# Six query and key projections of a stick-breaking attention: hi and lo tokens as one 512-column moving operand

## The chip, the core and the metric

The kernel runs on one NeuronCore of a Trainium2 chip. The metric is the device time of one execution in microseconds (us), lower is better. Engines are named as the profile names them: PE (TensorE matmuls), PEld (its weight loads), DVE (VectorE), ACT (ScalarE), SP (the queue that issues the weight transfers).

## The reference

A first block works on `x` (256 tokens, 1024 wide); two further layers of another kind follow. All of it is fp32. The part that the change touches is the projection of the normalised tokens to queries and keys:

```python
h = rms_norm(x, g_mix[l])
proj = h @ w_in[l]
c_h, c_b, c_c, sq, sk, sv, xq, gate_pre = jnp.split(proj, split_idx, axis=-1)
...
# stick-breaking attention, 16 heads of 64
z = jnp.einsum("bhqd,bhkd->bhqk", qb, kb).astype(jnp.float32) * scale   # scale = 0.125
log_beta = jax.nn.log_sigmoid(z)
log_1mb = jnp.where(past, jax.nn.log_sigmoid(-z), 0.0)
between = lax.cumsum(log_1mb, axis=3, reverse=True) - log_1mb
a = jnp.where(past, jnp.exp(log_beta + between), 0.0)
```

## The kernel before, in words

**Products.** Every fp32 matmul is made of three products of rounded parts: hi weights with hi tokens, lo weights with hi tokens, hi weights with lo tokens. The weights arrive in pieces of 1024 rows by 256 output columns, called halves here and `h` in the code. A half is one transfer of 1 MB into one of two slots of `raw`. ACT rounds it to `w_hi` (line 360), DVE forms `w_lo = raw - w_hi` (line 840), each into one of four ring slots. `split(0, h + 4)` in both engines' loops does this four halves ahead. SP issues the transfer of half l when DVE has formed `w_lo` of half l-2 (line 290).

**Order.** Halves 0 to 3 give the values, 4 to 11 (`SQK` to `CC`) the queries and keys in turn (even: queries, odd: keys), 12 to 23 the convolution's inputs. Every engine has its own program written out by hand, a loop over `h` with what is to be done beside each half; semaphores tie them together. Halves 4 and 5 use the raw tokens `Q_hi`, `Q_lo` and are scaled by DVE afterwards; halves 6 to 11 use the normalised tokens `H_hi`, `H_lo`.

**One half of a query or key on PE** (`rows_first`, line 1516): the weights are the stationary operand, the tokens the moving one, 256 columns. For each of 2 groups of 128 outputs and 8 pieces of 128 inputs there are three matmuls of 256 columns, 48 in all. Both groups share one bank of PSUM, `gps[:, h % 3]`. PE starts half h once `evac` has reached h-2, that is when the half that last used the bank has been copied out.

**Leaving PSUM.** One ACTIVATE of 128x512 (`evac`, line 376) copies a finished half to `qs` or `ks`; it stands in ACT's program ahead of the split of half h+4. Of halves 4 and 5 DVE does the copy, and ACT only raises the count `evac` by a `sem_inc`.

**Wide halves elsewhere.** In the feed-forward parts `rows_wide` (lines 1553 and 1557) already takes hi and lo tokens as one moving operand of 512 columns (`R_both`), with two banks for a half. What belongs together is then in one bank: hi products in columns 0 to 255, the lo tokens' products in columns 256 to 511. ACT copies the latter out (line 448), DVE adds the former (line 1034).

Of the kernel before, what the change touches and what calls it, by code (L numbers as in the profile page):

```python
# [20 lines left out]
P = 128  # L21
# [53 lines left out]
def build(nc, mem_t, x_t, x, w1, w2, rows1, rows2, rows3, par1, par2, con1, con2, turns, out):  # L75
    with ExitStack() as ctx:
        def sb(name, shape, dt=F32):
            return ctx.enter_context(nc.sbuf_tensor(name, shape, dt))

        def sem(name):  # L80
# [4 lines left out]
        w_hi = sb("w_hi", [P, 4, HALF], F32R)  # L85
        w_lo = sb("w_lo", [P, 4, HALF], F32R)

        H_hi, H_lo = sb("H_hi", [P, KT, T], F32R), sb("H_lo", [P, KT, T], F32R)
        R_both = sb("R_both", [P, KT, 2, T], F32R)
        R_hi, R_lo = R_both[:, :, 0, :], R_both[:, :, 1, :]  # L90
        Q_hi, Q_lo = sb("Q_hi", [P, KT, T], F32R), sb("Q_lo", [P, KT, T], F32R)
# [69 lines left out]
        raw_loaded = [sem("raw_loaded0"), sem("raw_loaded1")]  # L161
        x_piece = [sem(f"x_piece{i}") for i in range(4)]
        w_piece = [sem(f"w_piece{i}") for i in range(8)]
        names = """zeros front_xlo qk_scaled front_g front_hi front_lo vs_var vs_log vs_scale mem_loaded x_loaded par_loaded cst_loaded con_loaded lpar_loaded out_stored
            hi_ready lo_ready gemm_done evac act_step dve_step pads
            nsq nsum nvar nlog nrow nt nhi nlo resid acc_ready sqsum rows_loaded gn_row_loaded
            t_sq t_var t_log t_z t_tr summed
# [59 lines left out]
        def up_bank(m):  # L227

            return gps[:, m + 1, :]

        def wide_bank(a, nt):

# [119 lines left out]
        def _(act):  # L352
# [15 lines left out]
            def bank(l, ringsize=3):  # L368
                return gps[:, l % ringsize, :]

            def two(ap):
                return ap.rearrange("p (a t) -> p a t", a=2)
# [245 lines left out]
            staged_n = 0  # L618
            for h in range(SQK, FFN1):
                ps = bank(h)  # L620
                if h < SQK + 2:
                    act.wait_ge(s["qk_scaled"], h - SQK + 1)
                    act.sem_inc(s["evac"], 1)
                elif h < CC:
                    i = (h - SQK) // 2
                    if h % 2 == 0:
                        evac(qs[:, 2 * i:2 * i + 2, :], two(ps), h + 1, scale=0.125)
                    else:
                        evac(ks[:, 2 * i:2 * i + 2, :], two(ps), h + 1)
                elif h < CH:  # L630
                    i = h - CC
                    evac(u[:, 2 * i:2 * i + 2, 2:T + 2], two(ps), h + 1)
                elif h < MK:

                    if staged_n >= 2:
                        act.wait_ge(s["staged_free"], staged_n - 1)
                    evac(staged[:, staged_n % 2, :], ps, h + 1)
                    staged_n += 1
                elif h < MV or XQ <= h < XQ + 4:
                    if h in heads_ends:  # L640
                        n = heads_ends.index(h)
                        act.wait_ge(s["hd_tr"], n)
                        for m in range(2):
                            evac(heads[:, m, :], bank(h - 1 + m), h + 1)
                        head_squares(n)
                elif h < XQ:
                    if (h - MV) % 2:
                        for m in range(2):
                            evac(chunk(vx, m, (h - MV) // 2), bank(h - 1 + m), h + 1)
                elif h < WO1:  # L650
                    if (h - 36) % 4 == 1:
                        for m in range(2):
                            act.wait_ge(s["gemm_done"], h + 1)
                            act.wait_ge(s["staged_free"], staged_n + m - 1)
                            act.activation(gate[:, m, :], bank(h - 1 + m), ACT.Sigmoid).then_inc(s["evac"], 1)
                    elif (h - 36) % 4 == 3:
                        for m in range(2):
                            act.wait_ge(s["staged_free"], staged_n - 1)
                            evac(staged[:, m, :], bank(h - 1 + m), h + 1)
                            staged_n += 1  # L660
                if h in (GATED["conv"] + 4, WO1):
                    for m in range(2):
                        j = int(h == WO1)
                        act.wait_ge(s["mg_tr"], 2 * j + m + 1)
                        act.activation(operand(Q_hi, m, j), four(merged_turned(m, j)), ACT.Copy)\
                           .then_inc(s["mg_hi"], 1)
                if h == WO1:
                    act.preload_act_table_set("natural_log_exp_and_others")
                if h == MEM0:

                    act.wait_ge(s["mem_loaded"], 16)
                    for a in range(2):
                        squares(B7, B5, 2 * a, 2 * a + 2, s["nsq"])
                if h == MEM0 + 2:
                    rms_start(1)
                if SB0 <= h <= SB0 + 18:
                    t = (h - SB0) // 2
                    if h % 2 == 0:
                        if t >= 2:
                            sb_out(t - 2)  # L680
                        if t < SB_PAIRS:
                            sb_full(t)
                    elif t >= 1:
                        sb_copy(t - 1)
                if h + 4 < FFN1 + 2:
                    split(0, h + 4)
                if SB0 <= h <= SB0 + 18:
                    t = (h - SB0) // 2
                    if t < SB_PAIRS:
                        if h % 2 == 0:  # L690
                            sb_logs(t)
                        else:
                            sb_exp(t)
                if MEM0 + 2 <= h < MEM0 + 6:
                    rms_hi(1, h - MEM0 - 2, B5, R_hi)
                if h in heads_ends:
                    head_log(heads_ends.index(h))
                if CV0 <= h < CV0 + 4:

                    i = h - CV0  # L700
                    act.wait_ge(s["gemm_done"], XQ)
                    act.wait_ge(s["conv_y"], i + 1)
                    act.activation(R_hi[:, 2 * i:2 * i + 2, :], y[:, 2 * i:2 * i + 2, :], ACT.Copy)\
                       .then_inc(s["cv_hi"], 1)
                if h == CV0 + 3:
                    act.wait_ge(s["cv_lo"], 4)
                x0 = X0
                if x0 + 2 <= h < x0 + 2 + X_HEADS:
                    cx_out(h - x0 - 2)
                if x0 + 1 <= h < x0 + 1 + X_HEADS:  # L710
                    cx_copy(h - x0 - 1)
                if x0 <= h < x0 + X_HEADS:
                    cx_exp(h - x0)
                if h == GATED["x"] - 1:
                    act.wait_ge(s["gemm_done"], h + 1)
                    act.wait_ge(s["cx_oe"], X_HEADS)
                    for i in range(4):
                        act.activation(Q_hi[:, 2 * i:2 * i + 2, :], ox[:, 2 * i:2 * i + 2, :], ACT.Copy)\
                           .then_inc(s["ox_hi"], 1)
# [114 lines left out]
        def _(dve):  # L834
# [386 lines left out]
            dve.memset(u[:, :, 0:2], 0.0).then_inc(s["pads"], 1)  # L1221
            staged_n = 0
            for h in range(SQK, FFN1):
                if SB0 <= h <= SB0 + 18:
                    t = (h - SB0) // 2
                    if h % 2 == 0:
                        if t >= 2:
                            sb_out(t - 2)
                        if t < SB_PAIRS:
                            sb_masked(t)  # L1230
                    elif t < SB_PAIRS:
                        sb_arg(t)
# [276 lines left out]
        def _(pe):  # L1509
# [25 lines left out]
            def rows_first(h0, l, bank_, op_hi, op_lo, split_count=None):  # L1535
# [6 lines left out]
                        ins = rows_part(l, bank_, op_hi, op_lo, (nt,), range(KT))  # L1542
                ins.then_inc(s["gemm_done"], 1)

            def rows_wide(h0, l, a):

                r = ring(l)
                pe.wait_ge(s["lo_ready"], h0 + (l + 1))
                for nt in range(2):
                    b = wide_bank(a, nt)  # L1550
                    for k in range(KT):
                        c = k * 256 + nt * P
                        pe.matmul(b, w_hi[:, r, c:c + P], R_both[:, k, :, :].rearrange("p i t -> p (i t)"),  # L1553
                                  start=(k == 0), stop=False, skip_group_check=True)
                    for k in range(KT):
                        c = k * 256 + nt * P
                        ins = pe.matmul(b[:, 0:T], w_lo[:, r, c:c + P], R_hi[:, k, :],  # L1557
                                        start=False, stop=(k == KT - 1), skip_group_check=True)
                ins.then_inc(s["gemm_done"], 1)

            def tokens_part(l, out, m, g, op_hi, op_lo, start=False, stop=False, ks=range(4),
# [254 lines left out]
                              start=(m == 0 and j == 0), stop=(j == 1), skip_group_check=True)  # L1816
            sum_tiles(B5, (0, 1), aps[:, 3, 0:T], True, True).then_inc(s["nsum"], 1)
            for h in range(2, FFN1):
                if 3 <= h < WO1:
                    pe.wait_ge(s["evac"], h - 2)  # L1820
                if h < SQK:
                    tokens_half(0, h, h % 2, (2, 0), Q_hi, Q_lo, 1 if h == 2 else None)
                elif h < SQK + 2:
                    rows_first(0, h, h % 3, Q_hi, Q_lo)
                elif h < CC:
                    rows_first(0, h, h % 3, H_hi, H_lo, (s["nhi"], s["nlo"], 0, (1, 2, 3, 4)) if h == SQK + 2 else None)
                elif h < MK:
                    rows_first(0, h, h % 3, H_hi, H_lo)
                elif h < XQ:
# [344 lines left out]
```

## Time and profile before

| | |
|---|---|
| time, median of 3 runs | 1202.31 us (1202.1 to 1202.74) |
| time of the profiled execution | 1201.94 us |
| its span in the profile | 1200.2 us, 16502 instructions |
| PE busy | 1191.0 us (99%) |
| PEld, DVE, ACT busy | 1013.7 us (84%), 802.1 us (67%), 616.5 us (51%) |
| granted clock of TensorE, mean | 0.999 of full |
| DMA, mean | 183 GB/s |

The span is what the profiled execution's instructions cover. A matmul's row starts where the matmul starts, but its end is modelled and overlaps the next one's start, so a matmul's price in a stream is the distance between two starts and not its duration.

### The profile page before, as it was taken

The page shows a single profiled execution, that of the slowest core. Times are in us where ns is not written, and L with a number is a line of the kernel's source. Part 1 is how long each engine was busy: PE and PEld are TensorE (multiplying, and loading weights), DVE is VectorE, ACT ScalarE, POOL GpSimd, SP SyncE. Part 2 cuts the span into 40 slices and gives each one's busy share as a digit, 9 for nine tenths or more (in the row PEclk, how much of TensorE's full clock was granted, in tenths as well). Part 3 has the DMA queues.
Part 4 walks back from the last instruction along what each step waited for, and adds up shares of the span by engine and source line. Part 5 has one row for each costly group of instructions (what it writes and reads, how often), then busy time and mean ns, then how long its engine had stood idle before and what let it go on. Part 6 is the DMA issues. An engine that isn't in the chain of part 4 may idle for free.

```text
span 1200.2 us, 16502 instructions
## 1 busy us (share of the span) xinstructions
PE 1191.0 (99%) x6500; PEld 1013.7 (84%) x6500; DVE 802.1 (67%) x952; ACT 616.5 (51%) x769; POOL 3.5 (0%) x10
## 2 busy tenths in 40 slices
PE   9999999999999999999999999999999999999997
PEld 7999988888888888888888888888888888888886
DVE  6787986564656676656369697665675878766556
ACT  6567675564444555344356545443436654544441
POOL 0000000000000000000000000000000000000000
PEclk9999999999999999999999999999999999999999
DMA  7655354543555365555264446555536444565550
GB/s 263 227 190 176 135 182 148 207 172 140 220 200 190 115 236 201 184 203 182 105 246 176 149 177 214 207 199 186 191 124 246 169 155 176 188 228 180 194 192 36
DMA packets 34490, 219.25 MB, mean 183 GB/s; under 512 B 4080, under 2 KB 6144, under 8 KB 9088
## 3 DMA queue, kind: packets, MB, share of 16 engines
q1 hardware_dynamic: 32704, 215.26, 50.2%
q0 software_dynamic: 640, 2.11, 0.5%
q10 hardware_dynamic: 1088, 1.05, 0.3%
q8 instruction: 43, 0.70, 0.2%
q14 instruction: 15, 0.12, 0.0%
HBM read 217.34 MB, written 1.06 MB: 182 GB/s over the span
## 4 chain that ended last, share of the span: by engine, by line
PE 97%; DVE 1%; DMA 1%; ACT 0%; issue 0%; SPq 0%; DVEq 0%
PE gps L1516 14%; PE gps L1553 13%; PE gps L1571 11%; PE gps L1580 11%; PE gps L1573 11%; PE aps L1573 8%; PE aps L1571 8%; PE aps L1580 8%; PE gps L1557 7%; DMA raw<-w 1%; PE aps L1598 1%; PE aps L1755 1%; PE aps L1779 1%; PE aps L1929 0%; PE aps L1717 0%; PE gps L1941 0%
## 5 line engine op out<-in xcount | busy, mean ns | idle before, releaser
L840 DVE TENSOR_TENSOR w_lo<-raw,w_hi 128x2048 fp32r<-128x2048 f32 x194 | 444.2, 2291 | 234.9 <-ACT w_hi L360 234.2
L360 ACT ACTIVATE w_hi<-raw 128x2048 fp32r<-128x2048 f32 x194 | 371.5, 1916 | 214.2 <-PE aps L1580 96.7
L1553 PE MATMUL gps<-R_both,w_hi 128*128 128x512 f32 x672 | 167.9, 392 | 0.0
L1571 PE MATMUL aps<-w_hi,Q_hi 128*128 128x512 f32 x416 | 162.2, 390 | 0.0
L1573 PE MATMUL aps<-w_lo,Q_hi 128*128 128x512 f32 x416 | 162.2, 390 | 0.0
L1553 PEld LDWEIGHTS gps<-R_both,w_hi 128*128 128x128 f32 x672 | 122.2, 189 | 22.7
L1571 PE MATMUL gps<-w_hi,H_hi 128*128 128x512 f32 x288 | 114.8, 399 | 0.0
L1573 PE MATMUL gps<-w_lo,H_hi 128*128 128x512 f32 x288 | 112.4, 390 | 0.0
L1580 PE MATMUL aps<-w_hi,Q_lo 128*128 128x512 f32 x416 | 111.5, 390 | 0.0
L1516 PE MATMUL gps<-H_hi,w_hi 128*128 128x256 f32 x416 | 110.0, 286 | 0.0
L1516 PE MATMUL gps<-H_hi,w_lo 128*128 128x256 f32 x416 | 108.5, 283 | 0.0
L1557 PEld LDWEIGHTS gps<-R_both,w_lo 128*128 128x128 f32 x672 | 91.7, 190 | 6.6
L1557 PE MATMUL gps<-R_both,w_lo 128*128 128x256 f32 x672 | 93.7, 282 | 0.0
L1573 PEld LDWEIGHTS aps<-w_lo,Q_hi 128*128 128x128 f32 x416 | 78.2, 188 | 15.7
L1580 PEld LDWEIGHTS aps<-w_hi,Q_lo 128*128 128x128 f32 x416 | 77.9, 188 | 16.0
L1571 PEld LDWEIGHTS aps<-w_hi,Q_hi 128*128 128x128 f32 x416 | 78.2, 188 | 15.5
L1516 PE MATMUL gps<-H_lo,w_hi 128*128 128x256 f32 x416 | 83.1, 283 | 0.0
L1516 PEld LDWEIGHTS gps<-H_hi,w_hi 128*128 128x128 f32 x416 | 79.6, 191 | 3.2 <-issue 3.0
L448 ACT ACTIVATE staged<-gps 128x256 f32<-128x256 f32 x84 | 27.7, 382 | 101.6 <-PE gps L1557 101.6
L1516 PEld LDWEIGHTS gps<-H_hi,w_lo 128*128 128x128 f32 x416 | 79.7, 192 | 0.1
L1580 PE MATMUL gps<-w_hi,H_lo 128*128 128x512 f32 x288 | 77.7, 391 | 0.0
L1571 PEld LDWEIGHTS gps<-w_hi,H_hi 128*128 128x128 f32 x288 | 54.1, 188 | 14.3 <-issue 3.5
(252 smaller groups left out, 1561.6 us busy)
## 6 DMA issues: line engine op xcount, KB each, us to landing
raw<-w SPq DMA_DIRECT2D x194, 1024.0 KB, 4.8
B<-rows SPq DMA_DIRECT2D x4, 1024.0 KB, 4.5
raw<-w SPq DMA_DIRECT2D x8, 256.0 KB, 6.8
B<-turns POOLq DMA_DIRECT2D x4, 512.0 KB, 7.2
B<-x_t ACTq DMA_DIRECT2D x4, 256.0 KB, 5.6
B<-mem_t SPq DMA_DIRECT2D x1, 1024.0 KB, 8.7
B<-x SPq DMA_DIRECT2D x1, 1024.0 KB, 6.9
out<-B SPq DMA_DIRECT2D x4, 256.0 KB, 2.0
```

The source lines that it names most:

```text
L360: act.activation(w_hi[:, ring(l), :], raw[:, raw_slot(l), :], ACT.Copy)\
L448: act.activation(staged[:, a, nt * T:(nt + 1) * T], wide_bank(a, nt)[:, T:2 * T], ACT.Copy)\
L840: dve.tensor_tensor(w_lo[:, ring(l), :], raw[:, raw_slot(l), :], w_hi[:, ring(l), :].bitcast(F32), ALU.subtract)\
L1516: return pe.matmul(gps[:, bank_, nt * T:(nt + 1) * T], w[:, r, c:c + P], op[:, k, :], start=start, stop=stop, skip_group_check=True)
L1553: pe.matmul(b, w_hi[:, r, c:c + P], R_both[:, k, :, :].rearrange("p i t -> p (i t)"), start=(k == 0), stop=False, skip_group_check=True)
L1557: ins = pe.matmul(b[:, 0:T], w_lo[:, r, c:c + P], R_hi[:, k, :], start=False, stop=(k == KT - 1), skip_group_check=True)
L1571: pe.matmul(out, x, w_hi[:, r, c], start=(start and k == ks[0]), stop=False, skip_group_check=resumed)
L1573: pe.matmul(out, x, w_lo[:, r, c], start=False, stop=False, skip_group_check=resumed)
L1580: ins = pe.matmul(out, op_lo[:, 4 * g + k, rows], w_hi[:, r, c], start=False, stop=(stop and k == ks[-1]), skip_group_check=resumed)
L1598: ins = pe.transpose(turned(m, j)[:, k * P:(k + 1) * P], chunk(src, m, j)[:, k * P:(k + 1) * P], ident)
L1755: ins = pe.matmul(aps[:, h % 2, t * T:(t + 1) * T], qx[:, 2 * h + j, t * P:(t + 1) * P], kx[:, 2 * h + j, :], start=(j == 0), stop=(j == 1))
L1779: ins = pe.matmul(aps[:, 2, j * T:(j + 1) * T], vx[:, m, c:c + P], xpt[:, m * T:(m + 1) * T], start=(m == 0), stop=(m == 1))
```

## The change

`H_hi` and `H_lo` become the two parts of one tile `H_both`, laid out as `R_both` is. Halves 6 to 11 no longer run through `rows_first` but through `scores_wide`: 16 matmuls of 512 columns (hi weights with hi and lo tokens) and 16 of 256 (lo weights with hi tokens). A half has two banks: even halves `gps` 0 and 1, odd halves 2 and 3. ACT copies the lo columns of each bank to `qs` or `ks` (two ACTIVATEs of 128x256, count `qk_low`), then DVE adds the hi columns of the bank (two SCALAR_TENSOR_TENSORs of 128x256, count `qk_wide`). PE waits on `qk_wide` before it writes a pair of banks again.

```diff
+        H_both = sb("H_both", [P, KT, 2, T], F32R)
+        H_hi, H_lo = H_both[:, :, 0, :], H_both[:, :, 1, :]
...
 (ACT)       for h in range(SQK, FFN1):
                 ps = bank(h)
+                if SQK + 3 <= h <= CC:
+                    act.wait_ge(s["qk_wide"], 2 * (h - SQK - 2))
+                    act.sem_inc(s["evac"], 1)
                 if h < SQK + 2:
                     act.wait_ge(s["qk_scaled"], h - SQK + 1)
                     act.sem_inc(s["evac"], 1)
                 elif h < CC:
-                        evac(qs[:, 2 * i:2 * i + 2, :], two(ps), h + 1, scale=0.125)
-                        evac(ks[:, 2 * i:2 * i + 2, :], two(ps), h + 1)
+                    act.wait_ge(s["gemm_done"], h + 1)
+                    for nt in range(2):
+                        act.activation(qk_tile(h, nt), qk_bank(h, nt)[:, T:2 * T], ACT.Copy,
+                                       scale=(0.125, 1.0)[h % 2]).then_inc(s["qk_low"], 1)
...
 (DVE)       for h in range(SQK, FFN1):
+                if SQK + 2 <= h < CC:
+                    for nt in range(2):
+                        dve.wait_ge(s["qk_low"], 2 * (h - SQK - 2) + nt + 1)
+                        dve.scalar_tensor_tensor(qk_tile(h, nt), qk_bank(h, nt)[:, 0:T], (0.125, 1.0)[h % 2],
+                                                 qk_tile(h, nt), ALU.mult, ALU.add).then_inc(s["qk_wide"], 1)
...
 (PE)
+            def scores_wide(h):
+                pe.wait_ge(s["lo_ready"], h + 1)
+                if h == SQK + 2:
+                    for k in range(KT):
+                        if k % 2 == 0:
+                            pe.wait_ge(s["nlo"], k // 2 + 1)
+                        for nt in range(2):
+                            wide_hi(h, qk_bank(h, nt), nt, k, H_both)
+                    for nt in range(2):
+                        ins = wide_lo(h, qk_bank(h, nt), nt, H_both)
+                else:
+                    for nt in range(2):
+                        for k in range(KT):
+                            wide_hi(h, qk_bank(h, nt), nt, k, H_both)
+                        ins = wide_lo(h, qk_bank(h, nt), nt, H_both)
                 ins.then_inc(s["gemm_done"], 1)
...
-                if 3 <= h < WO1:
+                if SQK + 2 <= h < SQK + 4:
+                    pe.wait_ge(s["evac"], h - 1)
+                elif SQK + 4 <= h <= CC:
+                    pe.wait_ge(s["qk_wide"], 2 * (h - SQK - 3) if h < CC else 10)
+                elif 3 <= h < WO1:
                     pe.wait_ge(s["evac"], h - 2)
...
-                    rows_first(0, h, h % 3, H_hi, H_lo, (s["nhi"], s["nlo"], 0, (1, 2, 3, 4)) if h == SQK + 2 else None)
+                    scores_wide(h)
```

**DVE's program around half 6.** `B` stands for `qs` and `ks` here and for the squares of the memory tokens, `w_lo` is the low part of the weights. Before, from the memset that follows the split of half 7; the two splits are those of halves 8 and 9:

```order
L1221 MEMSET B 128x8x2 [waits nlo]
L840 TENSOR_TENSOR w_lo<-raw,w_hi 128x2048 [waits hi_ready] x2
L868 TENSOR_TENSOR B<-B 128x1024 [waits nsq]
L870 TENSOR_TENSOR B<-B 128x512 [waits dve_step]
L840 TENSOR_TENSOR w_lo<-raw,w_hi 128x2048 [waits hi_ready] x2
```

And of the change at the same place:

```order
L1233 MEMSET B 128x8x2 [waits nlo]
L852 TENSOR_TENSOR w_lo<-raw,w_hi 128x2048 [waits hi_ready] x2
L1239 SCALAR_TENSOR_TENSOR B<-gps,B 128x256 [waits qk_low] x2
L880 TENSOR_TENSOR B<-B 128x1024 [waits nsq]
L882 TENSOR_TENSOR B<-B 128x512 [waits dve_step]
L852 TENSOR_TENSOR w_lo<-raw,w_hi 128x2048 [waits hi_ready]
L1239 SCALAR_TENSOR_TENSOR B<-gps,B 128x256 [waits qk_low] x2
L852 TENSOR_TENSOR w_lo<-raw,w_hi 128x2048 [waits hi_ready]
```

The sum of half 6 stands behind the splits of halves 8 and 9, that of half 7 behind the split of half 10; each later sum also stands ahead of the split of the half four on.

**PE's program, halves 7 to 9.** Before; the three waits are the starts of halves 7, 8 and 9, and the rows between them, which repeat one pattern, are left out:

```order
L1516 MATMUL gps<-H_hi,w_hi 128x256 [waits lo_ready,evac]
...
L1516 MATMUL gps<-H_hi,w_hi 128x256 [waits lo_ready,evac]
...
L1626 MATMUL aps<-B,cst 128x256 [waits sqsum,nrow]
...
L1516 MATMUL gps<-H_hi,w_hi 128x256 [waits lo_ready,evac]
```

And of the change, halves 7 and 8:

```order
L1565 MATMUL gps<-H_both,w_hi 128x512 [waits lo_ready,evac]
L1565 MATMUL gps<-H_both,w_hi 128x512 x7
L1572 MATMUL gps<-H_both,w_lo 128x256 x8
L1565 MATMUL gps<-H_both,w_hi 128x512 x8
L1572 MATMUL gps<-H_both,w_lo 128x256 x8
L1565 MATMUL gps<-H_both,w_hi 128x512 [waits lo_ready,qk_wide]
L1565 MATMUL gps<-H_both,w_hi 128x512 x7
L1572 MATMUL gps<-H_both,w_lo 128x256 x8
L1565 MATMUL gps<-H_both,w_hi 128x512 x8
L1572 MATMUL gps<-H_both,w_lo 128x256 x8
```

The start of half 8 hangs on `qk_wide` of half 6 where it hung on `evac` of half 5.

## Rows read from the trace of the kernel before

**Rows 1.** The page: busy time of each engine; chain that ended last, by engine

```profile
PE 1191.0 (99%) x6500; PEld 1013.7 (84%) x6500; DVE 802.1 (67%) x952; ACT 616.5 (51%) x769; POOL 3.5 (0%) x10
PE 97%; DVE 1%; DMA 1%; ACT 0%; issue 0%; SPq 0%; DVEq 0%
```

**Rows 2.** Waits of PE: us in total, times, longest

```profile
PE aps L1808 <- DVE staged L1182: 1.2, 1, 1.2
PE gps L1571 <- DVE w_lo L840: 0.3, 1, 0.3
```

**Rows 3.** Timeline of PE: starts of halves 6 and 8; what follows halves 8 and 10

```profile
43.84 0.28 PE L1516 MATMUL gps<-H_hi,w_hi 128*128 128x256 f32 x1
...
55.36 0.28 PE L1516 MATMUL gps<-H_hi,w_hi 128*128 128x256 f32 x1
...
61.12 1.02 PE L1626 MATMUL aps<-B,cst 128*128 128x256 f32 x4
...
73.58 0.50 PE L1704 MATMUL aps<-B 64*128 64x128 f32 x4
```

**Rows 4.** Timeline of PE: a wide half of the feed-forward part

```profile
420.88 1.98 PE L1553 MATMUL gps<-R_both,w_hi 128*128 128x512 f32 x8
422.69 1.12 PE L1557 MATMUL gps<-R_both,w_lo 128*128 128x256 f32 x8
423.64 2.00 PE L1553 MATMUL gps<-R_both,w_hi 128*128 128x512 f32 x8
```

**Rows 5.** Timeline of DVE: splits of halves 9 to 13, one sum of squares

```profile
54.48 2.29 DVE L840 TENSOR_TENSOR w_lo<-raw,w_hi 128x2048 fp32r<-128x2048 f32 x1 [1.36 <-ACT w_hi L360]
56.85 1.23 DVE L868 TENSOR_TENSOR B<-B 128x1024 f32<-128x1024 f32 x1
...
60.04 2.29 DVE L840 TENSOR_TENSOR w_lo<-raw,w_hi 128x2048 fp32r<-128x2048 f32 x1 [1.23 <-ACT w_hi L360]
64.41 2.29 DVE L840 TENSOR_TENSOR w_lo<-raw,w_hi 128x2048 fp32r<-128x2048 f32 x1 [2.07 <-ACT w_hi L360]
...
70.22 2.29 DVE L840 TENSOR_TENSOR w_lo<-raw,w_hi 128x2048 fp32r<-128x2048 f32 x1
...
73.82 2.29 DVE L840 TENSOR_TENSOR w_lo<-raw,w_hi 128x2048 fp32r<-128x2048 f32 x1
```

**Rows 6.** Timeline of ACT: splits of halves 8 and 9, evacuation of half 6

```profile
48.87 1.92 ACT L360 ACTIVATE w_hi<-raw 128x2048 fp32r<-128x2048 f32 x1 [4.77 <-DMA raw<-w]
52.53 1.92 ACT L360 ACTIVATE w_hi<-raw 128x2048 fp32r<-128x2048 f32 x1 [1.74 <-DMA raw<-w]
54.35 0.58 ACT L376 ACTIVATE B<-gps 128x512 f32<-128x512 f32 x1
```

**Rows 7.** SP's issue of half 9's transfer; time to landing of raw's transfers

```profile
47.70 0.33 SPq L290 DMA_DIRECT2D raw<-w  x1
DMA to landing us min/median/max: 4.3/4.8/9.3
```

**Rows 8.** Timeline: two evacuations and two additions of a wide half

```profile
429.85 0.66 ACT L448 ACTIVATE staged<-gps 128x256 f32<-128x256 f32 x2
432.21 0.75 DVE L1034 TENSOR_TENSOR staged<-staged,gps 128x256 f32<-128x256 f32 x2
```

**Rows 9.** Timeline: a split of DVE, and PE's first two matmuls behind it

```profile
18.25 2.29 DVE L840 TENSOR_TENSOR w_lo<-raw,w_hi 128x2048 fp32r<-128x2048 f32 x1
...
20.59 0.50 PE L1571 MATMUL gps<-w_hi,Q_hi 128*128 128x512 f32 x1 [0.27 <-DVE w_lo L840]
20.93 0.40 PE L1573 MATMUL gps<-w_lo,Q_hi 128*128 128x512 f32 x1
```

**Rows 10.** The last matmul; then stretches: busy times, PEclk, DMA share, GB/s

```profile
1192.79 0.39 PE L1580 MATMUL aps<-w_hi,Q_lo 128*128 128x512 f32 x1
1194.00:1196.00 2.00, 0.00 (x0) 0.00 (x0) 1.86 (x7) 0.41 (x2) 0.00 (x0) 1.00 0.00 0
1196.00:1198.00 2.00, 0.00 (x0) 0.00 (x0) 1.67 (x3) 0.00 (x0) 0.00 (x0) 0.83 0.35 131
```

More of the change, by code:

```diff
@@ L86, in build @@
         w_lo = sb("w_lo", [P, 4, HALF], F32R)
-        H_hi, H_lo = sb("H_hi", [P, KT, T], F32R), sb("H_lo", [P, KT, T], F32R)
+        H_both = sb("H_both", [P, KT, 2, T], F32R)
+        H_hi, H_lo = H_both[:, :, 0, :], H_both[:, :, 1, :]
         R_both = sb("R_both", [P, KT, 2, T], F32R)
@@ L163, in build @@
         w_piece = [sem(f"w_piece{i}") for i in range(8)]
-        names = """zeros front_xlo qk_scaled front_g front_hi front_lo vs_var vs_log vs_scale mem_loaded x_loaded par_loaded cst_loaded con_loaded lpar_loaded out_stored
+        names = """qk_low qk_wide zeros front_xlo qk_scaled front_g front_hi front_lo vs_var vs_log vs_scale mem_loaded x_loaded par_loaded cst_loaded con_loaded lpar_loaded out_stored
             hi_ready lo_ready gemm_done evac act_step dve_step pads
@@ L229, in up_bank, with qk_tile, qk_bank @@
             return gps[:, m + 1, :]
+        def qk_tile(h, nt):
+            return (qs, ks)[h % 2][:, 2 * ((h - SQK) // 2) + nt, :]
+        def qk_bank(h, nt):
+            return gps[:, 2 * (h % 2) + nt, :]
         def wide_bank(a, nt):
@@ L624, in _ @@
                 elif h < CC:
-                    i = (h - SQK) // 2
-                    if h % 2 == 0:
-                        evac(qs[:, 2 * i:2 * i + 2, :], two(ps), h + 1, scale=0.125)
-                    else:
-                        evac(ks[:, 2 * i:2 * i + 2, :], two(ps), h + 1)
+                    act.wait_ge(s["gemm_done"], h + 1)
+                    for nt in range(2):
+                        act.activation(qk_tile(h, nt), qk_bank(h, nt)[:, T:2 * T], ACT.Copy,
+                                       scale=(0.125, 1.0)[h % 2]).then_inc(s["qk_low"], 1)
                 elif h < CH:
@@ L1543, in rows_first, with wide_hi, wide_lo @@
                 ins.then_inc(s["gemm_done"], 1)
+            def wide_hi(l, b, nt, k, both):
+                c = k * 256 + nt * P
+                pe.matmul(b, w_hi[:, ring(l), c:c + P], both[:, k, :, :].rearrange("p i t -> p (i t)"),
+                          start=(k == 0), stop=False, skip_group_check=True)
+            def wide_lo(l, b, nt, both):
+                for k in range(KT):
+                    c = k * 256 + nt * P
+                    ins = pe.matmul(b[:, 0:T], w_lo[:, ring(l), c:c + P], both[:, k, 0, :],
+                                    start=False, stop=(k == KT - 1), skip_group_check=True)
+                return ins
             def rows_wide(h0, l, a):
-                r = ring(l)
                 pe.wait_ge(s["lo_ready"], h0 + (l + 1))
@@ L1551, in rows_wide @@
                     for k in range(KT):
-                        c = k * 256 + nt * P
-                        pe.matmul(b, w_hi[:, r, c:c + P], R_both[:, k, :, :].rearrange("p i t -> p (i t)"),
-                                  start=(k == 0), stop=False, skip_group_check=True)
-                    for k in range(KT):
-                        c = k * 256 + nt * P
-                        ins = pe.matmul(b[:, 0:T], w_lo[:, r, c:c + P], R_hi[:, k, :],
-                                        start=False, stop=(k == KT - 1), skip_group_check=True)
+                        wide_hi(l, b, nt, k, R_both)
+                    ins = wide_lo(l, b, nt, R_both)
+                ins.then_inc(s["gemm_done"], 1)
+            def scores_wide(h):
+                pe.wait_ge(s["lo_ready"], h + 1)
+                if h == SQK + 2:
+                    for k in range(KT):
+                        if k % 2 == 0:
[9 more added lines that the diff above has]
+                        ins = wide_lo(h, qk_bank(h, nt), nt, H_both)
                 ins.then_inc(s["gemm_done"], 1)
```

## The prediction

> **What bounds the kernel now.** I read the page first: PE is busy for 99% of the span and makes up 97% of the chain that ended last, the chain of waits back from the last instruction [rows 1]. Then PE's waits: the longest is 1.2 us at the very start, the next 0.3 us [rows 2], and the last matmul starts at 1192.79 [rows 10], so the rest of the span is a tail of DVE and the output. PE is a gapless stream. Whatever makes this stream shorter or puts a hole into it moves the end by as much, since nothing behind it waits for anything else. So two questions remain: how much shorter six halves become, and whether PE has to wait where it did not.
>
> **What the matmuls give.** The timeline shows half 6 starting at 43.84, half 8 at 55.36 and the next work after half 8 at 61.12 [rows 3]: three halves in 17.28 us, 5.76 us each, or 120 ns for each of the 48 matmuls of 256 columns. A wide half is in the trace too, in the feed-forward part: eight matmuls of 512 columns from 420.88 to 422.69 (226 ns each), eight of 256 until 423.64 (119 ns each) [rows 4]. One group of 128 outputs takes 2.76 us, a half 5.52 us. The change turns each pair of 256-column matmuls (240 ns) into one of 512 (226 ns), 16 times per half: 0.24 us a half, 1.44 us over six halves. That is the whole possible gain, because the number of streamed columns stays at 12,288.
>
> Here a rule speaks against the change. In the Trainium skill, "TensorE: Matmul & The Clock Gate", section "Wait — 56ns, not 53.3ns?", a warm matmul's distance to the next is given as its columns at 2.4 GHz and about 2.5 ns. By that, merging two matmuls saves only 2.5 ns, an estimate of 0.24 us for all 96 merges, and the end would be 1.2 us later than by the rows. The rows differ from it (120 ns for 256 columns), so the rows decide here.
>
> **What the new wait costs.** PE may start half 8 only when DVE has added up half 6, because both use banks 0 and 1. Before, half 8 needed the copy of half 5, long done. I follow each engine.
>
> PE: halves 6 and 7 take 5.52 us each from 43.84, so PE is ready for half 8 at 54.88. (Half 7 also waits for ACT's `sem_inc`, which stands behind the split of half 8, 48.87 to 50.79 [rows 6]. Taken at the start of that split it costs nothing; taken at its end half 7 would run from 50.8 to 56.4. The wait that follows ends later than both, so the choice does not move half 8.)
>
> ACT: its copy of half 6 stands behind the split of half 9, which in turn waited for its transfer until 52.53; the copy started at 54.35 [rows 6]. That transfer was issued at 47.70 and took 4.8 us, the median [rows 7]. None of this hangs on how fast PE is, so it stays. Two copies of 128x256 take 0.66 us [rows 8] for the 0.58 us of one [rows 6], so the first half's columns are there near 54.7, the second's near 55.0.
>
> DVE: in its order the sum of half 6 stands behind the split of half 9, from 54.48 to 56.77 [rows 5]. Only then come the two new instructions. The nearest operation in the trace is the addition of a bank's half to a copy in SBUF in the wide halves, 0.75 us for two [rows 8]. It can't be free, as DVE works in program order; the dear end is a DVE instruction of twice the two's size, 128x1024 in 1.23 us [rows 5], half a us more. I take 0.75, the row of the nearest operation and shape. So the sum is ready at 57.5.
>
> PE restarts about 0.05 us behind that: after an earlier wait, on a split of DVE that ended at 18.25 + 2.29 = 20.54, it started at 20.59, and the second matmul came 0.34 us behind the first instead of 0.23 [rows 9], another 0.11 us. Half 8 so runs as if it had begun at 57.68 instead of 55.36: 2.3 us later than before, and PE stands idle for 2.7 us.
>
> **Does it happen again?** Half 9 needs the sum of half 7, which stands behind DVE's split of half 10. That split waits for ACT and, through it, a transfer; it stays at 60.04 to 62.33 [rows 5], since the sum of half 6 and the sums of squares (56.85 before, 0.8 us later now) fill idle time ahead of it. The sum of half 7 is ready at 63.1. PE reaches half 9 at 57.68 + 5.52 + 0.9 for the matmuls at line 1626 [rows 3] = 64.1: 1.0 us to spare. Half 10: split at 64.41, ends 66.7, sum ready 67.4, PE there at 69.6. Half 11: the split at 70.22 ends 72.5, 0.75 later now, and the sum 0.75 after that makes 74.0; PE is there at 76.0, behind the scores that followed half 10 at 73.58 [rows 3]. Half 12: the split at 73.82 ends at 76.1, three sums of 0.75 make 78.4, PE comes at 81.5. No further stall. These six pairs of sums add 4.5 us to DVE, which is idle 1 to 2 us ahead of most splits here [rows 5]; that idle time is the cover. If it were gone, `w_lo` of the halves 10 to 15 would be late, but each is ready several us before PE needs it. ACT's waits for `qk_wide` ask for sums of one half earlier, done by then. SP's queue moves only where `w_lo` moves, from half 12 on by 0.75 us, with three halves of PE's time to spare. The rounded tokens of half 6 are no new wait: lo parts are written before PE's stretch for the later pieces.
>
> **The sum.** +2.3 us at half 8, then four halves (8 to 11) shorter by 0.24: -0.96. The gain of halves 6 and 7 is inside the stall. Together +1.3 us. The profiled execution was 1201.94 (span 1200.2 and 1.7 around it), so it would be 1203.3; the median of the runs shown is 0.4 higher, and 1202.31 + 1.3 = 1203.6 is my forecast. It is 0.11% slower, and about 0.2% (2.4 us) is what a measurement of this kernel can tell from no change.
>
> **The rivals.**
> - *No stall, the full gain.* If the copy and the sum of half 6 were done by 54.9, the end would be 1.44 us earlier: 1200.9. For it speaks only that PE never waited here before; against it that DVE's split alone ends at 56.77. The transfer of half 9 would have to land 2.6 us sooner, in 2.2 us, with 4.3 the shortest of the trace [rows 7]. Chance 0.08, mostly for an error in my reading of the order.
> - *A later transfer (slower than can be taken for no change).* The stall's end hangs on the landing of half 9, then 1.92 us of ACT, 2.29 us of DVE and the sum, all in a row: each us by which it lands later is a us more. From 1.1 us on, a landing after 5.9 us, the result passes +2.4 us; the longest in the trace is 9.3 us [rows 7], which would give +5.8, or 1208.1. A late half 10 would use up the 1.0 us of half 9 likewise. Against it: this very transfer was at the median. At 1.4 us of lateness it is 1205.0. Chance 0.09.
> - *The clock falls in the stall.* The granted clock is full until 1196 at least, 2.8 us behind the end of the last matmul (1193.18), and lower in the stretch after [rows 10]. A hole of 2.7 us in a busy stream is just short of what is shown to be harmless. If the clock fell to 1.2 GHz, a half of 5.52 us at that level would cost 5.5 us more: 1209. The Trainium skill ("TensorE: Matmul & The Clock Gate", section "HAM oscillation — how this bites in real kernels") tells of kernels whose clock drops in waits between groups of matmuls. Chance 0.03.
> - *The merge gives nothing* (spacing as bound by loads or reads here): the stall without the 0.96, +2.3 us, 1204.6. Against it: the same operand shapes, in the feed-forward part [rows 4]. Chance 0.04.
>
> **How the numbers follow.** The forecast has 0.74; 0.02 stay for something faster that I do not see. The forecast's own range comes from a landing at 4.3 us (-0.5), the dear end of the sum (+0.5) and half a us of spread either way: 1202.6 to 1204.6. For 8 in 10 I reach a little to both sides, toward the full gain's 1200.9 at the low end and to a transfer that is 1.4 us late at the high end: 1201.3 to 1205.0. Faster by over 0.2% would need 2.4 us where 1.44 is the whole gain: only the unseen 0.02. Slower by over 0.2%: the late transfer, the clock, and 0.01 for the upper edge of the last rival, 0.13. The rest is 0.85.
>
> **What would show it.** In the changed kernel's profile: starts of the new 512-column matmuls 226 ns apart; one PE wait of 2.5 to 3 us at half 8, released by DVE's sum, near 57.5; no wait at halves 9 to 12; the scores after half 10 about 1.5 us later than 73.58; the end 1.3 us later. I am wrong if DVE's sum of half 6 precedes 56.7, if PE waits at half 9 or 11 too, or if PE finds idle time later in which the delay vanishes.

## The result

The changed kernel takes 1204.97 us in the median of 11 runs (1203.18 to 1209.06), the kernel before 1202.31 us (1201.84 to 1202.74, also 11 runs). The medians are 2.7 us apart, 0.22%, where 1.3 us or 0.11% was forecast. The ratio over all runs is 1.0024, with a 95% interval of 1.0016 to 1.0031. The kernel is slower, by more than the noise, where a smaller loss was forecast and "no change that can be told" had the best chance. The profiled execution took 1205.2 us with a span of 1203.4 us, 3.2 us more than the span of before.

The page, busy times and the chain that ended last, which answer to [rows 1]:

```profile
PE 1191.3 (99%) x6404; PEld 1009.7 (84%) x6404; DVE 805.9 (67%) x964; ACT 616.6 (51%) x775; POOL 3.5 (0%) x10
PE 93%; DMA 3%; DVE 2%; ACT 1%; issue 0%; SPq 0%; DVEq 0%; ACTq 0%
```

PE has 96 matmuls fewer (16 merges in each of six halves), DVE 12 instructions more, ACT 6 more. The chain stays on PE for less of the span, 93% where it was 97%; transfers are 3% where they were 1%, DVE and ACT together 3% where they were 1%. So somewhere PE waited for them. The view of PE's waits (us in total, times, longest) says where, against [rows 2]:

```profile
PE gps L1565 <- DVE B L1239: 2.3, 1, 2.3
PE aps L1851 <- DVE staged L1194: 1.2, 1, 1.2
```

One new wait of any size, on DVE's sum (line 1239), once. (Three short ones, 1.0 us together, end before 21 us, in code that the change leaves alone; half 6 starts 0.1 us later than before.) PE's timeline around it, from half 6 on, as [rows 3] show it for before:

```profile
43.94 3.82 PE L1565 MATMUL gps<-H_both,w_hi 128*128 128x512 f32 x16
47.59 2.08 PE L1572 MATMUL gps<-H_both,w_lo 128*128 128x256 f32 x16
49.50 2.00 PE L1565 MATMUL gps<-H_both,w_hi 128*128 128x512 f32 x8
...
57.57 2.54 PE L1565 MATMUL gps<-H_both,w_hi 128*128 128x512 f32 x8 [2.32 <-DVE B L1239]
59.91 1.91 PE L1572 MATMUL gps<-H_both,w_lo 128*128 128x256 f32 x8
61.62 2.43 PE L1565 MATMUL gps<-H_both,w_hi 128*128 128x512 f32 x8
63.88 1.11 PE L1572 MATMUL gps<-H_both,w_lo 128*128 128x256 f32 x8
64.84 1.02 PE L1669 MATMUL aps<-B,cst 128*128 128x256 f32 x4
...
68.49 2.00 PE L1565 MATMUL gps<-H_both,w_hi 128*128 128x512 f32 x8
...
71.28 2.00 PE L1565 MATMUL gps<-H_both,w_hi 128*128 128x512 f32 x8
...
74.08 2.00 PE L1565 MATMUL gps<-H_both,w_hi 128*128 128x512 f32 x8
...
76.96 0.50 PE L1747 MATMUL aps<-B 64*128 64x128 f32 x4
```

Half 8 starts at 57.57, as forecast, and then takes 7.27 us (to 64.84) where a wide half takes 5.59 us (two groups of outputs, as from 68.49 over 71.28 to 74.08). The reason is in the view by stretches (its columns: length, busy times of PE, PEld, DVE, ACT and POOL, then the granted clock, DMA share and GB/s):

```profile
58.00:59.00 1.00, 1.00 (x6) 0.81 (x5) 0.96 (x2) 1.00 (x1) 0.00 (x0) 1.00 0.70 180
59.00:60.00 1.00, 1.00 (x5) 0.77 (x4) 0.71 (x2) 1.00 (x3) 0.00 (x0) 0.54 1.03 434
60.00:61.00 1.00, 1.00 (x7) 1.00 (x6) 1.00 (x1) 0.17 (x1) 0.00 (x0) 0.50 0.96 401
61.00:62.00 1.00, 1.00 (x5) 0.95 (x5) 1.00 (x2) 0.12 (x1) 0.00 (x0) 0.50 0.11 41
62.00:63.00 1.00, 1.00 (x5) 0.77 (x4) 0.62 (x2) 1.00 (x1) 0.00 (x0) 0.75 0.00 0
63.00:64.00 1.00, 1.00 (x7) 0.82 (x5) 0.17 (x1) 0.80 (x1) 0.00 (x0) 1.00 0.80 147
```

After the 2.3 us hole PE worked on at full clock for 1.5 us and then at 1.2 GHz, the lower of the two levels, for 3.4 us (a mean of 0.54 over 1 us is 0.92 us at 0.5, one of 0.75 is 0.5 us: 0.92 + 1 + 1 + 0.5). Half of that is lost: 1.7 us. Before, the clock was full here, and PE had no hole:

```profile
57.00:60.00 3.00, 3.00 (x27) 3.00 (x26) 1.77 (x2) 1.91 (x2) 0.00 (x0) 1.00 0.82 265
```

What held the sum back, in the chain of this kernel over the hole:

```profile
52.61 1.93 ACT w_hi L369
...
54.56 2.29 DVE w_lo L852
56.85 0.68 DVE B L1239 x2
...
57.57 2.54 PE gps L1565 x8
```

The split of half 9 on ACT, then on DVE, then the two instructions of the sum, then PE. The account of the span: half 8 starts 57.57 - 55.36 = 2.2 us later, the lower clock takes 1.7 us, and halves 8 to 11 are shorter by 0.17 us each, 0.7 together. That makes 3.2 us, and 3.2 is measured between the two profiled executions. (The medians are 2.7 us apart; the profiled execution of before was one of its faster ones.)

### The profile page after: what moved, and what is told of

Its sections match the earlier page's. It is cut to its first block, busy times and chain, and to the rows that moved or that the text cites. A ratio compares the mean times of both kernels' runs of the same rounds, so it can differ in the third digit from the quotient of the medians.

```text
span 1203.4 us, 16334 instructions
## 1 busy us (share of the span) xinstructions
PE 1191.3 (99%) x6404; PEld 1009.7 (84%) x6404; DVE 805.9 (67%) x964; ACT 616.6 (51%) x775; POOL 3.5 (0%) x10
## 4 chain that ended last, share of the span: by engine, by line
PE 93%; DMA 3%; DVE 2%; ACT 1%; issue 0%; SPq 0%; DVEq 0%; ACTq 0%
PE gps L1565 14%; PE gps L1614 11%; PE gps L1616 10%; PE gps L1623 10%; PE gps L1533 9%; PE aps L1616 8%; PE aps L1614 8%; PE aps L1623 8%; PE gps L1572 7%; DMA raw<-w 3%; DVE w_lo L852 1%; ACT w_hi L369 1%; PE aps L1641 1%; PE aps L1798 1%; PE aps L1822 1%; PE aps L1976 0%
## 5 line engine op out<-in xcount | busy, mean ns | idle before, releaser
L1533 PE MATMUL gps<-H_both,w_hi 128*128 128x256 f32 x640 | 119.1, 285 | 0.0
L1614 PE MATMUL gps<-w_hi,H_both 128*128 128x512 f32 x288 | 114.8, 399 | 0.0
L1616 PE MATMUL gps<-w_lo,H_both 128*128 128x512 f32 x288 | 112.5, 390 | 0.0
L1533 PEld LDWEIGHTS gps<-H_both,w_hi 128*128 128x128 f32 x640 | 100.8, 191 | 2.8 <-issue 2.3
L1533 PE MATMUL gps<-H_both,w_lo 128*128 128x256 f32 x320 | 83.5, 283 | 0.0
L1623 PE MATMUL gps<-w_hi,H_both 128*128 128x512 f32 x288 | 77.7, 392 | 0.0
L1614 PEld LDWEIGHTS gps<-w_hi,H_both 128*128 128x128 f32 x288 | 54.1, 188 | 14.3 <-issue 3.5
L1616 PEld LDWEIGHTS gps<-w_lo,H_both 128*128 128x128 f32 x288 | 54.1, 188 | 10.6
L1623 PEld LDWEIGHTS gps<-w_hi,H_both 128*128 128x128 f32 x288 | 53.6, 188 | 11.2 <-DVE H_both L924 0.2
```

What stands on the lines that cost most here:

```text
L1533: return pe.matmul(gps[:, bank_, nt * T:(nt + 1) * T], w[:, r, c:c + P], op[:, k, :], start=start, stop=stop, skip_group_check=True)
L1614: pe.matmul(out, x, w_hi[:, r, c], start=(start and k == ks[0]), stop=False, skip_group_check=resumed)
L1616: pe.matmul(out, x, w_lo[:, r, c], start=False, stop=False, skip_group_check=resumed)
L1623: ins = pe.matmul(out, op_lo[:, 4 * g + k, rows], w_hi[:, r, c], start=False, stop=(stop and k == ks[-1]), skip_group_check=resumed)
```

## Experiments

Two questions were open. Is the loss the hole and the clock and nothing else? And does the clock fall because PE stands idle, or because of something in the wide matmuls? The runs of one batch share 27 runs of the kernel before: median 1202.36 us in the first batch (e1 to e4), 1202.29 us in the second (e5 to e7). Where nothing else is said, an experiment has 11 runs. Ratios and intervals are those of the runs, and so differ a little from the ratio of the medians.

**e2_hole_filled: PE busy during the wait.**

```diff
+FILL = 10
...
                 elif SQK + 4 <= h <= CC:
+                    if h == SQK + 4:
+                        for i in range(FILL):
+                            pe.matmul(aps[:, 1, :], H_both[:, 0, 0, 0:P],
+                                      H_both[:, 0, :, :].rearrange("p i t -> p (i t)"),
+                                      start=True, stop=True, skip_group_check=True)
                     pe.wait_ge(s["qk_wide"], 2 * (h - SQK - 3) if h < CC else 10)
```

> The changed kernel, with ten more matmuls of 512 columns (results unused, a bank that nobody needs then) between halves 7 and 8, where PE stands idle. They take 2.26 us and the sum of half 6 comes when it came before. Theory (the fall of the clock is caused by PE's idle time): same wait for the sum, so half 8 starts at 57.6 as in the changed kernel, but no fall of the clock; 1203.6, with little spread between runs. Rival (the clock falls for another reason, or the loss is the wait alone): 1205.0 and the same spread as the changed kernel, 1203.2 to 1209.

Measured: 1203.57 us (1203.08 to 1207.41), ratio 1.0013 [1.0004, 1.0022]. PE's timeline:

```profile
55.02 2.46 PE L1868 MATMUL aps<-H_both 128*128 128x512 f32 x10
57.45 2.11 PE L1566 MATMUL gps<-H_both,w_hi 128*128 128x512 f32 x8
59.40 1.11 PE L1573 MATMUL gps<-H_both,w_lo 128*128 128x256 f32 x8
60.35 2.00 PE L1566 MATMUL gps<-H_both,w_hi 128*128 128x512 f32 x8
62.19 1.11 PE L1573 MATMUL gps<-H_both,w_lo 128*128 128x256 f32 x8
63.14 1.02 PE L1670 MATMUL aps<-B,cst 128*128 128x256 f32 x4
```

Half 8 starts where it did in the changed kernel (57.45), but takes 5.69 us and not 7.27, and by the medians the end comes 1.4 us sooner. Unused work makes the changed kernel faster, though it stays slower than the kernel before. Ten of these eleven runs lie at 1203.88 us or lower, ten of the eleven of the changed kernel at 1204.55 or higher, so the two do not overlap but for one run of each. The wait itself costs what was forecast for it; the rest of the loss goes when PE is kept busy, so it was PE's idle time that brought the fall of the clock. The spread, which was expected to be little, has one run at 1207.41 us with a mean granted clock of 0.996 (the others have 0.998 or 0.999). The kernel before has such a run too, one in the 27 of the second batch, at 1206.02 us and 0.995. So one outlier of that size says nothing of this hole.

**e3_narrow_hole_short and e4_narrow_hole_long: holes in the kernel before, nothing wide.**

```diff
                 if 3 <= h < WO1:
                     pe.wait_ge(s["evac"], h - 2)
+                if h == SQK + 4:
+                    pe.wait_ge(s["lo_ready"], SQK + 6)
```

That is e3. In e4 the last line is `pe.wait_ge(s["sqsum"], 2)`.

> The kernel before, with nothing wide; PE's half 8 waits for w_lo of half 9 (ready at 56.8, where half 8 began at 55.36), an artificial hole of 1.4 us. Theory (a hole costs its length, a fall of the clock comes on top only when the hole is long enough): 1202.3 + 1.4 = 1203.7 if the clock does not fall; with a fall 1205.4. Rival (a hole of this size is swallowed later by PE): 1202.3.

> The kernel before, with nothing wide; PE's half 8 waits for DVE's sums of squares (ready at 58.8), an artificial hole of 3.4 us. Theory: 1202.3 + 3.4 = 1205.7 without a fall of the clock, 1207.4 with one; I expect the fall in nearly every run, and a granted clock below that of the kernel before. Rival (the fall in the changed kernel comes from the wide matmuls and not from idle time): 1205.7 with the clock of the kernel before.

Measured: e3 1203.77 us (1203.36 to 1204.69), ratio 1.0011 [1.0002, 1.002]; e4 1207.62 us (five runs: 1205.96 to 1209.57), ratio 1.0042 [1.0028, 1.0056]. Chains of PE over the holes, first e3, then e4 (the view names no releaser for these two waits and calls them "issue"):

```profile
53.98 2.16 PE gps L1516 x18
56.13 1.36 issue
57.49 5.62 PE gps L1516 x45
```

```profile
56.47 3.42 issue
59.89 8.13 PE gps L1516 x44
```

And the stretches, the first of e3 behind its hole, then those of e4:

```profile
60.00:62.00 2.00, 2.00 (x19) 2.00 (x19) 1.10 (x1) 1.36 (x2) 0.00 (x0) 1.00 0.88 365
```

```profile
58.00:60.00 2.00, 0.11 (x1) 0.14 (x1) 1.97 (x3) 2.00 (x2) 0.00 (x0) 0.75 0.63 115
60.00:62.00 2.00, 2.00 (x10) 2.00 (x11) 1.99 (x1) 0.14 (x1) 0.00 (x0) 0.50 0.93 393
62.00:64.00 2.00, 2.00 (x11) 2.00 (x11) 0.00 (x0) 0.66 (x1) 0.00 (x0) 0.50 0.49 94
64.00:66.00 2.00, 2.00 (x12) 2.00 (x11) 0.72 (x1) 1.25 (x1) 0.00 (x0) 0.54 0.96 393
```

A hole of 1.36 us costs 1.4 us and the next half runs as ever. A hole of 3.4 us costs 5.3 us in the median; what is left beside its own length is 1.9 us. The profiled execution, the slowest of the five, shows where such a rest comes from: the clock is at the lower level from 59.0 to 65.8, and half 8 takes 8.45 us between starts (59.89 to 68.34) where a half takes 5.76, 2.7 us lost. Here the clock fell while PE still stood idle, 2.5 us behind the end of its last matmul. The one run at 1205.96 is 3.6 us above the kernel before and has a mean granted clock of 0.999, the other four have 0.996 to 0.998: in it the clock did not fall. So the fall needs no wide matmuls, and at this place it came behind holes of 2.3 and 3.4 us, not behind one of 1.4.

**e7_hole_part_filled: the hole cut to 1.3 us, the wait kept.** The edit of e2 with four matmuls for ten.

> The changed kernel with four unused matmuls of 512 columns (0.9 us) ahead of PE's wait at half 8, so that the hole shrinks from 2.5 to about 1.5 us while half 8 still starts at 57.6. Theory (what counts for the clock is how long PE is idle; 1.4 us in the narrow kernel did no harm): no fall, 1203.6, as with ten. Rival (any wait for the sum brings the fall, however long): 1205.0.

Measured: 1203.25 us (1202.93 to 1204.33), ratio 1.0005 [0.9996, 1.0014]. PE's timeline and the stretches of the profiled execution:

```profile
56.13 1.09 PE L1868 MATMUL aps<-H_both 128*128 128x512 f32 x4
58.56 2.14 PE L1566 MATMUL gps<-H_both,w_hi 128*128 128x512 f32 x8 [1.34 <-DVE B L1240]
```

```profile
57.00:60.00 3.00, 1.66 (x7) 1.20 (x7) 2.97 (x5) 3.00 (x5) 0.00 (x0) 1.00 0.28 57
60.00:63.00 3.00, 3.00 (x19) 2.62 (x18) 3.00 (x4) 0.58 (x3) 0.00 (x0) 1.00 0.70 295
```

A hole of 1.34 us in the changed kernel leaves the clock alone, like that of 1.36 in the narrow one. But this execution, the slowest of the eleven, has a fall elsewhere, near the start, where PE stands idle for a short time in some executions of these kernels:

```profile
PE gps L1615 <- DVE w_lo L853: 0.7, 1, 0.7
18.00:22.00 4.00, 3.21 (x16) 2.54 (x16) 2.81 (x4) 2.49 (x4) 0.00 (x0) 0.88 0.48 154
22.00:26.00 4.00, 4.00 (x14) 3.12 (x14) 3.58 (x7) 2.11 (x5) 0.00 (x0) 0.69 0.60 248
```

PE restarts behind this wait of 0.67 us at 20.84, and from 21.0 to 24.5 us the clock is at the lower level; half 8 starts 1 us later than in the changed kernel. The changed kernel's own profiled execution waits 0.42 us at that place and the clock stays full. So the length of one hole does not settle alone whether the clock falls; what does is open.

**e1_sum_early: the sum of half 6 ahead of the split of half 9.** On ACT and on DVE (`qk_copy` is the wait on `gemm_done` and the two ACTIVATEs; ACT's copies of the other halves stay where they are):

```diff
 (ACT)           if h < SQK + 2:
                     act.wait_ge(s["qk_scaled"], h - SQK + 1)
                     act.sem_inc(s["evac"], 1)
+                    if h == SQK + 1:
+                        qk_copy(SQK + 2)
...
 (DVE)
-                if SQK + 2 <= h < CC:
+                for g in ((SQK + 2,) if h == SQK + 1 else (h,) if SQK + 3 <= h < CC else ()):
                     for nt in range(2):
```

> The changed kernel, with ACT's copies and DVE's sum of half 6 ahead of the split of half 9 instead of behind it. Theory (the whole loss is the one hole in PE's stream at half 8, 2.3 us, and the half at the lower clock behind it, about 1.7 us, against 1.44 us of merged matmuls): half 6 ends near 49.5, its sum is done near 51, long before PE needs banks 0 and 1 at about 55; no wait of PE at half 8, no fall of the clock, and the time is that of the kernel before less 1.4 us, 1200.9. Rival (the two-bank layout itself costs, by later waits at halves 9 to 12 or by DVE's 12 extra instructions): still above 1202.3.

Measured: 1202.41 us (1201.43 to 1203.41), ratio 1.0002 [0.9993, 1.0011]. The hole at half 8 is gone and with it the loss, but the gain did not come: 1200.9 was expected. The rival of the expectation, a later wait at halves 9 to 12, is what happened. PE's waits and timeline:

```profile
PE gps L1571 <- DVE B L1245: 0.5, 1, 0.5
```

```profile
55.09 2.00 PE L1571 MATMUL gps<-H_both,w_hi 128*128 128x512 f32 x8
...
62.23 2.11 PE L1571 MATMUL gps<-H_both,w_hi 128*128 128x512 f32 x8 [0.53 <-DVE B L1245]
```

The wait has moved to half 9: the sum of half 7 stands behind the split of half 10 and is ready near 62.2, while PE, no longer held up at half 8, could start at 61.3 (55.09, then 5.59 for half 8 and 0.67 for the four matmuls that follow it). The 1.0 us to spare at half 9 had been counted with a PE that is late; without the first hole there is none. The profiled execution has a hole of only 0.5 us and is the fastest of the eleven (1201.43); that the others have longer ones is likely but not shown.

**e5_three_sums_early and e6_all_sums_early: three or six sums one split sooner.**

```diff
+def sums_at(h):
+    out = []
+    if SQK + 2 <= h < CC and h not in EARLY:
+        out.append(h)
+    if h + 1 in EARLY:
+        out.append(h + 1)
+    return out
...
 (ACT)
+                if SQK < h < CC:
+                    for g in sums_at(h):
+                        qk_copy(g)
...
 (DVE)
-                if SQK + 2 <= h < CC:
+                for g in sums_at(h):
```

`EARLY` is (6, 7, 8) in e5 and (6, 7, 8, 9, 10, 11) in e6. Both places stand ahead of `split(0, h + 4)`.

> The changed kernel with ACT's copies and DVE's sums of halves 6, 7 and 8 each one split sooner (ahead of the splits of halves 9, 10 and 11). Theory (in the run before, with the sum of half 6 alone moved, the hole went to half 9, whose sum stands behind the split of half 10, and nothing else eats the gain): no wait of PE at halves 8 to 12, scores behind half 10 near 72.4, time 1202.3 - 1.4 = 1200.9, narrow spread. Rival (12 more DVE instructions and 6 more of ACT cost about a us elsewhere): 1202 or more with no hole in PE's stream at halves 8 to 12.

> The same with all six copies and sums one split sooner. Theory (only the place behind a split that waits for a transfer hurts; from half 9 on either place is in time): 1200.9, as with three. Rival (from half 9 on ACT and DVE now wait for PE's half itself, with a split of weights queued behind, so w_lo or the squares of the memory tokens come late): slower than with three, by a PE wait at half 9 to 15.

Measured: e5 1200.76 us (1200.55 to 1202.33), ratio 0.9986 [0.9977, 0.9995]; e6 1200.56 us (1200.29 to 1201.65), ratio 0.9984 [0.9975, 0.9993]. Both are faster than the kernel before, and their intervals exclude 1. DVE and PE in e5:

```profile
50.45 2.29 DVE L868 TENSOR_TENSOR w_lo<-raw,w_hi 128x2048 fp32r<-128x2048 f32 x1 [2.83 <-ACT w_hi L379]
52.66 0.75 DVE L1255 SCALAR_TENSOR_TENSOR B<-gps,B 128x256 f32<-128x256 f32 x2
54.48 2.29 DVE L868 TENSOR_TENSOR w_lo<-raw,w_hi 128x2048 fp32r<-128x2048 f32 x1 [1.06 <-ACT w_hi L379]
56.69 0.75 DVE L1255 SCALAR_TENSOR_TENSOR B<-gps,B 128x256 f32<-128x256 f32 x2
```

```profile
55.05 2.00 PE L1581 MATMUL gps<-H_both,w_hi 128*128 128x512 f32 x8
...
60.64 1.02 PE L1685 MATMUL aps<-B,cst 128*128 128x256 f32 x4
...
72.76 0.50 PE L1763 MATMUL aps<-B 64*128 64x128 f32 x4
```

The sum of half 6 now fills idle time ahead of the split of half 9, which still starts at 54.48, bound by its transfer. PE has no wait from half 6 to 12; the scores behind half 10 begin at 72.76 where they began at 73.58. With all six early nothing is gained or lost that could be told: where DVE waits for PE's own half (1.66 us ahead of the sum of half 9 in e6), the splits behind have slack enough.

## Why the prediction was wrong

- **What bounds the kernel, and where the change would hurt: right.** One new PE wait, at half 8, on the sum of half 6, held back by the split of half 9 and its transfer. PE restarted at 57.57, to the 0.1 us of the forecast. No wait came at halves 9 to 12.
- **The step that failed is the clock: the sum has no term for it, and the rival "The clock falls in the stall" was given 0.03.** I read [rows 10] as a sign that 2.8 us of idle time do no harm. They only show when the clock fell after the end of the last matmul, where PE did no more work. In the changed kernel it fell 1.5 us after PE had resumed, and in e4 2.5 us behind the last matmul, sooner than the 2.8 us that I had taken for harmless. It cannot be inferred from one execution's tail that a hole of 2.3 us is safe. A fall was the likeliest case: nine of the eleven runs lie between 1204.55 and 1206.09 and only one at 1203.18, the time without a fall; the slowest is at 1209.06. That these nine all had one is read from their times, as only one trace is kept. The mean granted clock of each run fits but does not settle it: 0.997 or less in six of the eleven, 0.998 in the other five; of the 54 runs of the kernel before in the two batches only one is below 0.998.
- **The price in that rival was wrong too.** I took a whole half at 1.2 GHz, 5.5 us. Measured are 3.4 us at the lower level, 1.7 us lost in the profiled execution; by medians, the changed kernel less e2, 1.4 us. With the fall in the sum at the price that e2 gives afterwards, the forecast would have been 1203.6 + 1.4 = 1205.0. The Trainium skill ("TensorE: Matmul & The Clock Gate", section "HAM oscillation — how this bites in real kernels") tells of waits between groups of matmuls behind which the clock is low. In its example these waits last about 3 to 5 us. The 3.4 us of e4 agree with that; the hole of 2.3 us is shorter than any of them and the clock fell all the same, so here the measurement goes beyond the page.
- **The wait alone was sized right**: half 8 starts 2.2 us later where 2.3 was forecast, and e2, which has the wait without the fall, takes 1203.57 us where 1203.6 was forecast.
- **The gain of a merge was oversized.** A wide half takes 5.59 us here, not the 5.52 read from [rows 4]; the eight 512-column matmuls start 1.84 us from the next group, not 1.81. That is 0.17 us a half, 1.0 us for six. e5 shows it in PE's stream (behind half 14, 98.38 against 99.35; the last matmuls start 1.2 us sooner) and 1.5 us in the medians; the other half us is not explained. The estimate that the prediction took from the Trainium skill ("TensorE: Matmul & The Clock Gate", section "Wait — 56ns, not 53.3ns?"), with a fixed 2.5 ns per matmul, gives 0.24 us for six halves: the rows are nearer. (The prediction says that the end would be 1.2 us later by it; its own sum counts four halves, so 0.8 would follow.)
- **"Does it happen again?" held only for the late PE.** The 1.0 us to spare at half 9 came from the hole ahead of it, as e1 shows.
- The range, 1201.3 to 1205.0, just holds the median, and that is luck: its upper edge came from a late transfer, and the transfer of half 9 was on time (ACT's split starts at 52.61, before 52.53). "The same" had 0.85, on the ground that 2.4 us (0.2%) is the least that can be told; the measured 2.7 us is beyond that.

## What to carry to other kernels

When a wait is put into PE's stream, count its length and then what the clock adds: here, at one place of the stream, a hole of 1.4 us cost its own length, one of 2.3 us 1.4 us more by the medians, one of 3.4 us 1.9 us more. That is no safe limit: in one execution the clock fell behind a hole of 0.67 us. When PSUM is freed by a pair of engines that also prepare weights in program order, put the evacuation ahead of whatever waits for a transfer, and not only for the half where the wait shows, since the next wait appears when the first is gone (here three halves had to move, and moving six gave no more). One outlier among many runs is no sign that a hole brought the clock down, as the kernel before has one too; that most runs lie higher than the hole explains is such a sign.

## What was unexpected in the hardware

In the changed kernel the clock fell not in the hole but after it: PE had worked again at full clock for 1.5 us (57.57 to about 59.1) before the lower level came, which stayed for 3.4 us while PE was busy throughout. In e4 it fell inside the hole, and the lower level stayed for 6.8 us. Ten matmuls whose results nobody reads, put into the hole, made the changed kernel 1.4 us faster. And e7's profiled execution has a stretch of 3.4 us at the lower level near 21 us, behind a hole of only 0.67 us and other short waits.
